# Decode samples' q, k, v from one stationary tile that holds high and low parts side by side

## The reference, cut to what matters

```python
h = (rms_norm(x, norm_g) * (1.0 + scale) + shift)
proj = h @ w_in
q = rms_norm(q.reshape(heads), q_gain[:, None, :]) * (HEAD_DIM ** -0.5)
k = rms_norm(k.reshape(heads), k_gain[:, None, :])
```

## Time and profile before

| | us |
|---|---|
| median of 3 runs | 2255.28 (2254.46 to 2255.65) |
| the profiled execution, its own time | 2255.71 |
| its span, first to last instruction | 2253.9 |
| TensorE matmul busy | 2184.0 (97%) |
| TensorE weight load busy | 2044.3 (91%) |
| VectorE busy | 828.9 (37%) |
| ScalarE busy | 584.7 (26%) |
| GpSimd busy | 240.1 (11%) |

### The profile page before, as it was taken

The page is one execution under the profiler, slowest core; times in us unless marked ns, Lnnn a source line. Parts: engine busy times, 40 slices in busy tenths (PEclk is TensorE's granted clock), DMA queues, the critical chain, the costliest instruction groups (busy, mean ns, idle before and its releaser), DMA issues. The chain is left out here.

```text
span 2253.9 us, 37021 instructions
## 1 busy us (share of the span) xinstructions
PE 2184.0 (97%) x12891; PEld 2044.3 (91%) x12891; DVE 828.9 (37%) x2244; ACT 584.7 (26%) x2140; POOL 240.1 (11%) x376
## 2 busy tenths in 40 slices
PE   7799999999999999999989999999999978999999
PEld 2599999999999999999979989999999977998897
DVE  3623233233333333333231234122221327666663
ACT  3523333333333333333341111111111123111010
POOL 1122121111111111111110000000000001000000
PEclk9899999999999999999999999999999988999999
DMA  9356657655645555454343333545323336444441
GB/s 336 120 184 217 198 188 220 202 176 172 191 151 187 164 170 174 139 184 140 106 137 118 112 116 110 190 141 187 101 96 98 111 124 230 164 167 142 141 131 52
DMA packets 252178, 354.05 MB, mean 157 GB/s; under 512 B 19597, under 2 KB 225685, under 8 KB 250615
## 3 DMA queue, kind: packets, MB, share of 16 engines
q1 hardware_dynamic: 207577, 309.82, 42.2%
q10 hardware_dynamic: 44454, 42.33, 5.8%
HBM read 256.52 MB, written 183.77 MB: 195 GB/s over the span
## 5 line engine op out<-in xcount | busy, mean ns | idle before, releaser
L979 PE MATMUL a_pp<-a_wH,hH 128*128 128x384 f32 (+1 forms) x1632 | 565.7, 347 | 11.4 <-DVE a_wL L1253 11.4
L981 PE MATMUL a_pp<-a_wH,hL 128*128 128x384 f32 (+1 forms) x1632 | 553.2, 339 | 0.0
L980 PE MATMUL a_pp<-a_wL,hH 128*128 128x384 f32 (+1 forms) x1632 | 551.4, 338 | 0.0
L979 PE MATMUL pp<-hH,wH 128*128 128x412 f32 (+1 forms) x1120 | 393.4, 351 | 5.9 <-DVE wL L669 5.9
L980 PE MATMUL pp<-hL,wH 128*128 128x412 f32 (+1 forms) x1120 | 391.7, 350 | 0.0
L981 PE MATMUL pp<-hH,wL 128*128 128x412 f32 (+1 forms) x1120 | 391.6, 350 | 0.0
L979 PEld LDWEIGHTS a_pp<-a_wH,hH 128*128 128x128 f32 (+1 forms) x1632 | 298.2, 183 | 18.9 <-DVE a_wL L1253 11.6
L980 PEld LDWEIGHTS a_pp<-a_wL,hH 128*128 128x128 f32 (+1 forms) x1632 | 298.3, 183 | 7.5
L981 PEld LDWEIGHTS a_pp<-a_wH,hL 128*128 128x128 f32 (+1 forms) x1632 | 297.4, 182 | 8.3
L1205 ACT ACTIVATE a_junk<-a_pp 128x128 f32<-128x128 f32 (+1 forms) x408 | 113.0, 277 | 631.5 <-PE a_pp L981 625.0
L1261 DVE TENSOR_SCALAR a_ms<-a_ss 128x2 f32<-128x2 f32 (+1 forms) x204 | 34.3, 168 | 640.9 <-ACT a_junk L1205 640.9
(11 more groups left out here) (195 smaller groups left out, 2850.3 us busy)
## 6 DMA issues: line engine op xcount, KB each, us to landing
out_dram<-in_state_kv_w_dram SPq DMA_DIRECT2D x64, 1023.5 KB, 5.9
qkv_dram<-qkv SPq DMA_DIRECT2D x192, 192.0 KB, 2.0
qkv_in<-qkv_dram SPq DMA_DIRECT2D x192, 192.0 KB, 2.7
w_first<-in_w_in_dram SPq DMA_DIRECT2D x46, 512.0 KB, 6.8
gl<-gT_dram SPq DMA_DIRECT2D x64, 264.0 KB, 3.8
gT_dram<-ost ACTq DMA_DIRECT2D x80, 206.0 KB, 2.6
out_dram<-in_state_kv_w_dram SPq DMA_DIRECT2D x8, 2044.0 KB, 10.5
o_dram<-ot ACTq DMA_DIRECT2D x192, 65.0 KB, 2.2
```

The source lines that it names most:

```text
L979: nc.tensor.matmul(out, sH, mH, start=(i == 0), stop=False)
L980: nc.tensor.matmul(out, sH, mL, start=False, stop=False)
L981: last = nc.tensor.matmul(out, sL, mH, start=False, stop=(i == len(terms) - 1))
```

## The change

For the step of the samples, the 24 matmuls become 16. A new tile `hs` holds, for each of the 8 slices of the contraction, 40 stationary columns: the samples' high parts in columns 0 to 7, zeros in 8 to 31, the remainders in 32 to 39. Two passes, over `wH` and over `wL`, give in PSUM rows 0 to 7 the high part times both halves of the weights, and in rows 32 to 39 the low part times both halves (so the product low times low, which was left out, is now in the sum). ScalarE copies rows 32 to 39 out to `s_low`, VectorE adds them to rows 0 to 7 into `s_sum`, and the squares, the copy of v and the normalisation read `s_sum` in place of PSUM. In `prepare` the tile is filled: a GpSimd memset of the zeros, a GpSimd copy of the high parts (placed ahead of the one into `hH`), a VectorE subtraction at the end. `hs_m` becomes another name of `hs_t`.

```diff
+LOW = 32
+        hs = keep_sb("hs", [P, KT, LOW + NS], F32R)
...
-        hs_m = sb("hs_m", [P, KT, NS])
         hs_t = sb("hs_t", [P, KT, NS])
+        hs_m = hs_t
...
                 nc.gpsimd.memset(mhalf[:, :], -0.5).then_inc(mhalf_ready, 1)
+                nc.gpsimd.memset(hs[:, :, NS:LOW].bitcast(F32), 0.0)
                 pool.wait_ge(ident_zero, 1)
...
                 pool.wait_ge(samp_step, 2)
+                nc.gpsimd.tensor_copy(hs[:, :, 0:NS], hs_t[:, :, :])
                 nc.gpsimd.tensor_copy(hH[:, :, SEQ:TT], hs_t[:, :, :]).then_inc(samp_hi, 1)
...
                 nc.vector.tensor_tensor(hL[:, :, SEQ:TT], hs_t[:, :, :], hH[:, :, SEQ:TT].bitcast(F32), ALU.subtract)
+                nc.vector.tensor_tensor(hs[:, :, LOW:], hs_t[:, :, :], hH[:, :, SEQ:TT].bitcast(F32), ALU.subtract)
...
+        s_low = sb("s_low", [NS, 3 * P])
+        s_sum = sb("s_all", [NS, 3 * P])
...
-                    src = pp[s % 2]
+                    src = pp[s % 2] if b < BLOCKS else s_sum
                     act.wait_ge(proj_done, s + 1)
+                    if b == SAMP:
+                        nc.scalar.activation(s_low[:, :], pp[s % 2][LOW:LOW + NS, 0:3 * P], ACT.Copy).then_inc(low_read, 1)
+                        act.wait_ge(samp_summed, s // UNIT + 1)
...
                 def mean(s):
                     rows = P if s % UNIT < BLOCKS else NS
+                    if rows == NS:
+                        dve.wait_ge(low_read, s // UNIT + 1)
+                        nc.vector.tensor_tensor(s_sum[:, :], pp[s % 2][0:NS, 0:3 * P], s_low[:, :], ALU.add).then_inc(samp_summed, 1)
...
                 def project(s):
                     u, b = divmod(s, UNIT)
-                    rows = P if b < BLOCKS else NS
-                    cols = tokens(b)
...
+                    if b == SAMP:
+                        for k in range(KT):
+                            nc.tensor.matmul(pp[s % 2][0:LOW + NS, 0:3 * P], hs[:, k, :], wH[u % 2][:, k, :], start=(k == 0), stop=False)
+                            last = nc.tensor.matmul(pp[s % 2][0:LOW + NS, 0:3 * P], hs[:, k, :], wL[u % 2][:, k, :], start=False, stop=(k == KT - 1))
+                        last.then_inc(proj_done, 1)
+                        return
+                    cols = slice(b * P, (b + 1) * P)
```

More of the change, by code:

```diff
@@ L142, in prepare @@
     w_ada_v = v["w_ada"][0].rearrange("(k p) c -> p k c", p=P)
-    gate_dram = v["gate_dram"]
+    gate_dram, hs = v["gate_dram"], v["hs"]
     NC = 1 + NS
@@ L998, in attend @@
 def attend(nc, scope, v):
-    hH, hL, ident = v["hH"], v["hL"], v["ident"]
+    hH, hL, hs, ident = v["hH"], v["hL"], v["hs"], v["ident"]
     w_in_v, o_dram, samp_dram, bulk, qkv_dram = v["w_in_v"], v["o_dram"], v["samp_dram"], v["bulk"], v["qkv_dram"]
@@ L1079, in attend @@
         w_hi, w_lo, next_in = sem("aw_hi"), sem("aw_lo"), sem("next_in")
+        low_read, samp_summed = sem("low_read"), sem("samp_summed")
         proj_done, squared, act_read, meaned, powered, qk_normed = (
@@ L1091, in three @@
             return ap.rearrange("p (i c) -> p i c", c=P)
-        def tokens(b):
-            return slice(SEQ, TT) if b == SAMP else slice(b * P, (b + 1) * P)
         with nc.Block() as block:
@@ L1321, in project @@
                         pe.wait_ge(qk_normed, s - 1)
+                    if b == SAMP:
[5 more added lines that the diff above has]
+                    cols = slice(b * P, (b + 1) * P)
                     split = (lambda k: pe.wait_ge(w_lo, u * KT + k + 1)) if b == 0 else None
-                    three_pass(nc, pp[s % 2][0:rows, 0:3 * P], [(hH[:, k, cols], hL[:, k, cols], wH[u % 2][:, k, :], wL[u % 2][:, k, :])
+                    three_pass(nc, pp[s % 2][:, 0:3 * P], [(hH[:, k, cols], hL[:, k, cols], wH[u % 2][:, k, :], wL[u % 2][:, k, :])
                                                                 for k in range(KT)], split).then_inc(proj_done, 1)
```

## The result

The changed kernel takes 2242.7 us (median of 4 runs, 2241.22 to 2242.98) against 2255.2: ratio 0.9944, 95% interval 0.9931 to 0.9958. That is 12.5 us less, where 15.4 was forecast; the time lies 2.8 us above the forecast 2239.9. The profiled execution took 2242.48 us, 13.2 less than that of before.

The account below looks back on a forecast made before the run. TensorE bounds the kernel, busy 1052.94 of 1053.00 us with projections. Terms: -15.29 - 0.35 + 0.05 + 0.20 = -15.4 us, from the median 2255.28 to 2239.9 us; range 2237.4 to 2245.3.

Parts of the forecast that it names:

- The removed matmuls: Samples' steps: eight fewer matmuls at 0.1738 us save 1.390 us a unit, counted in full in 11 units, 15.29 us.
- The 40 columns: Samples' steps: the 16 matmuls that stay cost the same with 40 stationary columns, at most 0.2 us more in all.
- The rival in which the weight load lies open: Samples' steps: loads of 40 columns not hidden, 0.48 us a unit, 5.3 us over 11 units, 2245.2 us; chance 0.04.
- The added chain: Samples' step: ScalarE's copy and VectorE's sum ahead of the squares take 1.05 us (bounds 0.9 and 1.8), hidden from TensorE.
- slack 1.6 us: Samples' step: with the chain, probabilities are copied by 507.97, and TensorE reaches its next `values` at 509.6.
- The last unit and the tail: Behind the last samples' step: 1.39 us earlier, stretched by 1.05, so the phase's end moves by -0.35 us.
- The preparing phase: Before the attention phase: 0.05 us for GpSimd's second copy and 0.20 for VectorE's last subtraction, 0.2 to 0.3 us longer.
- Another phase changes its length: Other phases, with the same instructions: a change in length there would show the prediction wrong; 0 us was forecast.
- The forecast's own band: Whole kernel: the matmuls count in full, 2239.9 us with 2237.8 to 2242 around it; chance 0.83.
- third: Samples' steps: chain over 2.65 us, or a late load in some units, gives back half, 7.7 us: 2247.6 us; chance 0.08.
- fourth rival: Samples' steps: the same wait in all units, large enough to be slower; at 5 us of chain 2265.9 us; chance 0.02.

Follow-up runs that it names:

- The fill alone: The kernel before, with the new tile allocated and filled in the preparing phase and never read: 2255.16 us, ratio 0.9998 (0.9988 to 1.0007) to the kernel before.

## Why the prediction was right, and where 3 us went

- **The removed matmuls** were priced right: 16.7 forecast for all twelve units, 16.6 measured in the profiled pair, and 0.176 us each when eight were put back. The clock at full level and the even spacing were enough to know this. That it agrees to 0.1 us is luck: in the second profile of the changed kernel the stretch is 0.9 us longer.
- **The 40 columns** cost nothing, as forecast: spacing 0.173 us. The rival in which the weight load lies open is refuted, and with it, for these loads, the rule that the prediction quoted from the Trainium skill, "TensorE: Matmul & The Clock Gate", section "Part 3: Packing small matmuls": loads of 115 ns to all rows of the array are hidden behind the matmuls.
- **The added chain** was forecast at 1.05 us and measured at 1.18: 1.09 for copy and sum, 0.09 for the two squares that now read SBUF (43 ns more each). Hidden, as forecast. The claim "slack 1.6 us" is wrong for the first unit, which has no attention parts. There the samples' bank, which the prediction put aside as "wanted only by the projection after the next", is wanted first, and some 0.5 us is left at 1.18 us of chain.
- **The last unit and the tail** is a mis-sized term: +1.04 in the stretch behind the last projection was forecast (1.39 shorter projection and -0.35 net), +1.44 was measured. 0.13 is the chain, 0.25 the landing of one load. So the twelfth unit's 1.39 us brought nothing.
- **The preparing phase**: +0.25 forecast. In the profiled pair +0.7, but the phase's end moves by itself: 94.8 and 96.7 us in two profiles of before, 95.5 to 97.9 in eight with this fill. The fill alone gives a ratio of 0.9998. Its size stays open within these 2 us; only the 0.14 us of the second subtraction is seen directly.
- **"Another phase changes its length"** was listed as something that would speak against the prediction, and it happened: +1.2 us in the two later phases (+1.7 against the second profile of the kernel before). The missing term is the clock behind each barrier. It was not foreseen at all, and it is the largest part of the 2.2 us between the profiled pair's 13.2 and the 15.4.
- **The range** held for a reason of its own. The forecast's own band ended at 2242, and the measured 2242.7 lies above it; the stated range reached to 2245.3 only because it took in the open weight load, which did not happen. That the time fell into that upper part of the range through the clock and the tail, which the forecast had not foreseen at this size, is luck.
- The third and fourth rival, a wait for ScalarE and VectorE, did not come true at 1.18 us of chain; first waits show at 2.7 us, and large ones at 5.3. The load that comes late, the other condition of the third, did happen outside the tail, but in one of the two profiles of the changed kernel and for 0.7 us only.

The sum as measured in the profiled pair: -16.59 + 1.44 + 0.73 + 1.19 = -13.23 us. Between the profiled pair's 13.2 and the medians' 12.5 lies the scatter of single executions.

## What to carry to other kernels

Where TensorE never waits, each of these matmuls of 384 moving columns cost 0.173 to 0.175 us, with 8, 40 or 128 stationary columns alike. Packing two operands side by side into one stationary tile and adding the two row groups afterwards saves a pass, if the engines behind have slack for one copy and one sum. Look separately at the last repetition, where no further work covers the lengthened chain, and at what is queued behind it: moving one load ahead of two stores took 1.3 to 1.5 us from the tail. When comparing kernels to a us, take the clock behind each barrier into the account, since two phases that weren't touched moved by up to 1 us each.

## What was not expected of the hardware

- The first 6 us of the third phase had a mean granted clock between 0.58 and 0.76 in the kernels of the table. With 1.5 us more work ahead of it, the clock came back at the same moment, 1072.0 us behind the start of the attention phase against 1072.0 to 1072.8, and from there to the end nothing of the 1.5 us was to be seen.
- A wait of 3.6 us in otherwise steady work was followed by TensorE's lower level (mean 0.85 over ten us); eight added copies of 0.48 us a unit cost 42 us in the phase where the waits add up to 25, and some 28 us at the lower level are most of the difference.
- ScalarE's square of 8x128 took 310 ns from SBUF, where from PSUM it had taken 267; its copy of 8x128 took 292 and 251.
